# Two-layer hybrid attention encoder: the low halves of 46 weight blocks are made by VectorE in one operation each, where GpSimd made them in four

## The reference, cut to what matters

```python
SEQ, D_MODEL, DEPTH, HEAD_DIM = 1024, 1024, 2, 64
def reference(x, w_in, ..., w_out, g_mix, g_mlp, w_up, w_down, g_final):
    for l in range(DEPTH):
        h = rmsnorm(x, g_mix[l])
        proj = h @ w_in[l]                              # 1024 x 1024 by 1024 x D_IN
        aq, ak, av, bq, bk, bv, cq, ck, cv, cf = split(proj)
        o_a = diff_attention(aq, ak, av, lam, ...)      # softmax(q1 k1) - lam softmax(q2 k2), 4 heads
        o_b = sliding_window_sink_attention(bq, bk, bv, sinks, ...)
        o_c = forgetting_attention(cq, ck, cv, log_sigmoid(cf + c_fbias[l]))
        x = x + concatenate([o_a, o_b, o_c]) @ w_out[l]
        h = rmsnorm(x, g_mlp[l])
        x = x + square(relu(h @ w_up[l])) @ w_down[l]
    return rmsnorm(x, g_final)
```

## Time and profile before

| | us |
|---|---|
| timed runs, median (lowest to highest) | 2525.82 (2523.96 to 2527.11) |
| the profiled execution's own time | 2525.3 |
| its span, first to last instruction | 2523.5 |
| PE busy (share of the span) | 2388.8 (95%) |
| DVE busy | 1707.2 (68%) |
| ACT busy | 1119.9 (44%) |
| POOL busy | 269.5 (11%) |

### The profile page before, as it was taken

How to read it: one execution, slowest core, us unless ns; L and a number is a source line. 1 busy time by engine, 2 the same in 40 slices (tenths; PEclk the granted TensorE clock), 3 DMA queues, 4 the chain that set the end, 5 groups by cost and what they waited for, 6 DMA issues and landing times.

```text
span 2523.5 us, 32747 instructions
## 1 busy us (share of the span) xinstructions
PE 2388.8 (95%) x11857; PEld 1936.7 (77%) x11857; DVE 1707.2 (68%) x3130; ACT 1119.9 (44%) x1984; POOL 269.5 (11%) x287
## 2 busy tenths in 40 slices
PE   7999899899899989999999989998999999799997
PEld 6877777678788877888878777776777888688886
DVE  5555666666877768888636556666577777697873
ACT  5554444553444433333436544454454444333333
POOL 1111011123000000000221111121220000000003
PEclk9999999999999999999999999999999999899999
DMA  5201011211344467868331000102114444787753
GB/s 171 76 26 26 18 26 34 67 51 48 117 145 144 152 216 247 270 191 263 126 88 30 26 26 18 34 26 67 59 42 159 142 154 157 239 274 237 222 178 98
DMA packets 289928, 296.06 MB, mean 117 GB/s; under 512 B 19510, under 2 KB 236640, under 8 KB 289512
## 3 DMA queue, kind: packets, MB, share of 16 engines
q1 hardware_dynamic: 284056, 278.24, 35.0%
q10 hardware_dynamic: 5712, 15.73, 1.6%
HBM read 212.10 MB, written 81.82 MB: 116 GB/s over the span
## 4 chain that ended last, share of the span: by engine, by line
PE 78%; DVE 8%; issue 4%; ACT 4%; DMA 2%; DVEq 2%; POOL 0%; SPq 0%; ACTq 0%; POOLq 0%
PE ps L1883 23%; PE ps L2150 19%; PE ps L2202 8%; PE ps L2203 8%; PE ps L2204 8%; PE ps L2016 3%; PE ps L1963 3%; PE ps L2046 2%; PE ps L2036 1%; DVE probs L1393 1%; ACT probs L1018 1%; DVE probs L1421 1%; ACT pt_both L1036 1%; PE ps L2048 1%; DMA b_saved<-v_tile 1%
## 5 line engine op out<-in xcount | busy, mean ns | idle before, releaser
L2202 PE MATMUL ps<-b_hi,d_hi 128*128 128x512 f32 x896 | 350.7, 391 | 10.7 <-DVE d_lo L1685 10.6
L1883 PE MATMUL ps<-wide_hi,w_hi 128*128 128x512 f32 x1024 | 339.5, 413 | 21.2 <-POOL w_lo L871 6.3
L2204 PE MATMUL ps<-b_hi,d_lo 128*128 128x512 f32 x896 | 349.9, 391 | 0.0
L2203 PE MATMUL ps<-b_lo,d_hi 128*128 128x512 f32 x896 | 349.9, 391 | 0.0
L1883 PE MATMUL ps<-wide_lo,w_hi 128*128 128x512 f32 x1024 | 321.6, 396 | 0.0
L1883 PE MATMUL ps<-wide_hi,w_lo 128*128 128x512 f32 x1024 | 319.2, 393 | 0.0
L1444 DVE TENSOR_TENSOR pt_both<-ps,pt_both 128x512 fp32r<-128x512 f32 (+3 forms) x216 | 126.4, 585 | 222.8 <-ACT pt_both L1036 222.0
L1140 ACT ACTIVATE d_hi<-d_raw 128x1024 fp32r<-128x1024 f32 x112 | 118.4, 1058 | 338.3 <-DVE d_raw L1674 110.8
L1036 ACT ACTIVATE pt_both<-ps 128x512 fp32r<-128x512 f32 (+3 forms) x216 | 110.4, 511 | 337.6 <-PE ps L2016 337.3
L871 POOL TENSOR_TENSOR w_lo<-w_raw,w_hi 128x256 fp32r<-128x256 f32 x216 | 164.4, 792 | 830.2 <-ACT w_hi L921 830.2
L1018 ACT ACTIVATE probs<-probs,neg_max,slope 128x256 f32<-128x256 f32 (+7 forms) x256 | 202.3, 791 | 95.3 <-DVE neg_max L1408 75.2
(11 more groups left out here) (204 smaller groups left out, 4471.6 us busy)
## 6 DMA issues: line engine op xcount, KB each, us to landing
b_raw<-b_saved SPq DMA_DIRECT2D x112, 512.0 KB, 6.6
d_raw<-in_w_down_dram SPq DMA_DIRECT2D x112, 512.0 KB, 6.3
a_raw<-in_w_up_dram SPq DMA_DIRECT2D x60, 512.0 KB, 4.2
b_saved<-c_rows SPq DMA_DIRECT2D x120, 256.0 KB, 4.4
w_raw<-in_w_in_dram SPq DMA_DIRECT2D x92, 256.0 KB, 3.3
b_saved<-far SPq DMA_DIRECT2D x32, 512.0 KB, 4.2
w_raw<-in_w_out_dram SPq DMA_DIRECT2D x36, 256.0 KB, 3.0
x_saved<-xt ACTq DMA_DIRECT2D x16, 512.0 KB, 2.6
```

The source lines that it names most:

```text
L1883: mm = T.matmul(ps[p][:, bass.ts(t, BANK)], w, h[:, bass.ts(t, BANK)], start=(start and n == 0), stop=(stop and n == 2))
L2202: T.matmul(out, w0, b0, start=first, stop=False)
L2203: T.matmul(out, w0, b1, start=False, stop=False)
L2204: mm = T.matmul(out, w1, b0, start=False, stop=last)
```

## The change

Blocks 6 to 26, 28 and 29 of each layer, 23 in each and 46 in all, leave POOL's list. DVE makes their low part at the end of the slot in which ACT makes the high part, behind `half_low` and the sums and ahead of the next slot's `biased_max`, in one operation of 128 x 1024. It waits for ACT's copy (`w_hi_done`). POOL keeps blocks 2 to 5 and `EXTRA`.

```diff
@@ POOL, once per layer
-                for n in range(2, IN):
+                for n in range(2, 6):
                     low_weights(n)
                 scale_head(0)
                 scale_head(1)
-                for n in range(OUT, OUT + 3):
-                    low_weights(n)
                 scale_head(2)
-                low_weights(OUT + 3)
                 pool.wait_ge(w_hi_done, LOADS * l + EXTRA + 1)
                 nc.gpsimd.tensor_tensor(xw_lo[:]..., w_raw[:, 0:2 * NPARTIAL], xw_hi[:]..., ALU.subtract).then_inc(w_split, 1)
-                low_weights(EXTRA + 1)
-                low_weights(EXTRA + 2)
                 norm_squares(2 * l)
@@ DVE, end of each slot, behind sum_values / fold_values
+                    for n in s.split:
+                        if n != EXTRA:
+                            split_load(l, n)
                     if l == 0 and t == NQ and s.first:
                         lambdas()
```

## The result

The changed kernel takes 2566.57 us (median of four runs, 2563.0 to 2567.76), against 2525.99 us of the kernel before, timed beside it. The ratio is 1.0159, 95% interval 1.0142 to 1.0177: 40.6 us slower. The forecast was 2554 us, 28 us slower, with a range to 2570: the direction and the place were right, the size was short by 12 us.

The account below looks back on a forecast made before the run. PE, busy 95%, was taken to bound the kernel. Waits of 13.6 us a layer made 27 us, plus 2 us for PE's clock: 29 us on 2525.3 gave 2554 us, range 2540 to 2570.

Parts of the forecast that it names:

- What bounds, and what can be gained: Whole kernel: PE bounds, busy 95%; PE waits for no low part that moves, so making it sooner gives nothing.
- The waits: DVE waits for ACT's copy in attention; PE loses 2.7, 2.7, 3.9, 1.7 us at blocks 17, 20, 23, 28; 27 us in all.
- The four small ones: Blocks 6, 10, 24, 26: copy ready or nearly so, DVE later by the operation; 2.6 us a layer, between 0 and 4.6.
- What the operation costs: Each moved subtraction on DVE in attention: 1.22 us, upper bound 2.30; 1.15 us net, 53 us of added DVE time.
- what POOL's silence gave back: Attention: fewer POOL collisions with DVE's small `neg_max` operation; counted as 0 in the sum, 6 us in the range.
- the clock's term: PE at half clock behind new gaps at blocks 17, 20, 23 in both layers: 2 us added, between 0 and 10.
- It fits into DVE's spare time: Rival: DVE's 187 us idle per attention absorbs 27 us of new work; no change, 2525 us; 6%.
- Faster by no collision: Rival: POOL no longer collides with DVE in attention, maxima come earlier; at most 6 us faster, 2519 us; 5%.
- In the path everywhere: Rival: all 46 operations cost PE their full 1.15 us, plus the waits; 2580 us and more; 6% above 2571.

Follow-up runs that it names:

- e_fill: The changed kernel plus 8, 20 and 9 matmuls nobody reads, in PE's gaps behind blocks 17, 23 and 24 of each layer: 2557.07 us, ratio 1.0111.
- e_only_four: The kernel before, with only blocks 17, 20, 23 and 28 of each layer made by DVE: 2557.8 us, ratio 1.0110 to the kernel before.
- e_four_back: The changed kernel, with blocks 17, 20, 23 and 28 of each layer given back to POOL: 2533.8 us, ratio 1.0019 to the kernel before.
- e_early: The kernel before, with only block 3 of each layer moved to DVE, between the gate's difference and its scan: 2517.4 us, ratio 0.9963.

## Why the prediction was right, and where it was not

**What bounds, and what can be gained.** Right. No moved low part had kept PE waiting, and making it faster gave nothing. The rule of the Trainium skill that an elementwise operation with two inputs belongs on VectorE (GPSIMD Engine Reference, 4.1 Engine selection) holds for the operation, 1.23 us against 3.2, and the kernel became 1.6% slower by following it.

**The waits.** Right, block by block. Block 17: forecast 2.7, measured 2.61. Block 20 the same. Block 23: 1.9 + 3.9 = 5.8 us of gaps forecast, 4.70 + 0.94 = 5.64 measured. Block 28: 1.7 forecast, 0.82 + 0.78 = 1.60 measured. The four small ones: forecast 2.6 us a layer; in the trace of the change PE's new idle time is 0.8 us behind block 10, 0.6 at block 24 and 1.2 behind block 26. At block 6 the rows were misread: ACT's copy comes 2.1 us after DVE, as late as at block 17, and it costs PE nothing. The whole: 27 us forecast, 25.7 measured.

**What the operation costs.** Right: it takes 1.23 us, and DVE's busy time rose by 47.3 us, which is 56.3 less 9. Of these 9, about 3 are the 0.07 us by which each overlaps the next one's start; the rest is what POOL's silence gave back, 4.8 of it on `neg_max`. Of that gift nothing can be seen in the time. POOL fell to 135 us and not to 124: the moved operations had taken 0.73 us each, and those that stayed are the slow ones.

**The step that failed** is the size of the clock's term: "I add 2 us, between 0 and 10". It measured 16.8 us between the two profiles, and 13 to 16 by the mean granted clock of the timed runs (0.977 against 0.982 to 0.983). That the time came out in the range owes something to luck: the waits were 1.3 us under the forecast and every other term at its middle, so a clock term some 3 us larger would have left it. Two things were wrong in it. I took the 3.4 us stretch of the earlier trace rows as the unit for every gap, at 1.7 us lost, and counted blocks 17, 20 and 23 alone. Laid side by side, PE's matmuls took 1.7 us longer behind block 17 in each layer, nothing behind block 20, 5.4 and 5.5 us from block 23 to behind block 24, 1.7 behind block 28 in layer 0, and 1.6 and 1.5 around 215.6 us and its twin, where no gap is new. And I took nearly all of it back by the argument that a slow PE lets DVE catch up; in `e_fill` this holds for a fifth at most (4.1 of 21.1 us at the filled places). By this the term should have stood at 10 or more with its end near 20.

**The rivals.** "It fits into DVE's spare time" asked for slack at four blocks; the gaps of the change and `e_only_four` show that there is too little. "Faster by no collision": the collisions went, the maximum from 716 to 231 ns, and the time rose. "In the path everywhere": `e_four_back` has 38 of the 46 for 0.19%. How the sum's gaps split into wait and operation the prediction did not say; alone, the operation cost more than I expected of it.

**Not shown:** which property of a gap brings the lower clock. Equal gaps were followed by it in one place or kernel and not in another: blocks 17 and 20, block 20 in the change and in `e_fill`, and the 1.79 us before 215.6 in both kernels and in `e_fill`.

## What to carry to other kernels

A helper's operation moved to another in-order engine takes its wait along, and everything behind it in that list inherits the wait; so read, for each place, when the operand is ready against when the engine arrives, and move the operation behind the next results that the bounding engine takes (here 0.26% instead of 1.59% for the same work). Move it at all only where the bounding engine waits for that very result: one block in each layer gave 0.4%, the 46 others together cost at each of the three places where they were tried. When new gaps open on PE, price the clock apart from the waits: the growth of PE's busy time at equal instruction counts is that price in the result, and here it was two fifths of the loss. Take it from more than one execution, or check it by the granted clock of the timed runs: between runs of one kernel it went from 0.979 to 0.986, which is 18 us.

## What the runs showed of the hardware

- PE's stretches at the lower of its two levels (granted clock 0.50) lasted 3.4, 6.8 or 10.3 us in the attention of the change, the longest behind the longest gap, and gaps of one size were followed by such a stretch in some places and not in others. Thirty-seven matmuls a layer that nobody reads, in three gaps, kept the clock at 1.00 over blocks 23 and 24 and gave 12 us in the kernel that has the gaps.
- The length of one POOL operation sets how long DVE can be held up. A DVE operation on 128x2 elements that takes 0.23 us took up to 0.72 us (0.83 in `e_early`) while POOL worked in 128x256 pieces (0.79 us each), up to 1.38 us when POOL worked in 128x1024 (2.47 us each), and 0.23 us at most when POOL was nearly silent. Larger operations show it too: a scan of 2.29 us alone took 2.68 beside the short pieces and 4.32 beside the long one, a combination of 1.15 us took 2.76. It goes both ways, as POOL's block beside that scan took 5.55 us for 2.8. Cutting POOL's work in four costs it 0.7 us a block in the mean and shields DVE. The Trainium skill says that the two engines' common port pair is an exclusive lock, held for a whole instruction (SBUF — State Buffer, SBUF: two separate sides); the maxima grow with POOL's operation as that would have it.
